# A two-layer diffusion backbone on one core: the opening's modulation rows turned on chip, wider weight runs, and small transfers moved later

## The reference, cut to what matters

```python
def layer(x, xc, c_act, cc_act, lp, cos, sin, with_ctx):
    mod = (c_act @ lp['w_mod'] + lp['b_mod']).reshape(c_act.shape[0], 1, 9, D_MODEL)
    modc = (cc_act @ lp['w_mod'] + lp['b_mod']).reshape(9, D_MODEL)
    m = lambda i: mod[:, :, i]
    mc = lambda i: modc[i]
    ada = lambda t, g, shift, scale: rms_norm(t, g) * (1 + scale) + shift
    x = x + 0.5 * m(2) * ffn(ada(x, lp['norm_ffn1'], m(0), m(1)), 'ffn1')
    xc = xc + 0.5 * mc(2) * ffn(ada(xc, lp['norm_ffn1'], mc(0), mc(1)), 'ffn1')
...
```

## Time and profile before

| | before |
|---|---|
| median of 3 executions | 2305.62 us |
| the profiled execution, its own time | 2308.61 us |
| its span in the profile | 2306.9 us |
| PE busy | 2197.4 us (95%) |
| DVE, ACT, POOL busy | 1472.5, 1006.0, 566.4 us |
| mean DMA rate over the span | 147 GB/s |

### The profile page before, as it was taken

One profiled execution on the slowest core, in us unless ns is written; L12 is line 12 of the kernel. 1 busy time (PEld: TensorE's weight loads), 2 busy tenths in 40 slices (PEclk: granted clock), 3 DMA queues, 4 the chain that ended last, 5 costly groups with the idle time before them and its releaser, 6 DMA issues. The chain is left out here.

```text
span 2306.9 us, 32947 instructions
## 1 busy us (share of the span) xinstructions
PE 2197.4 (95%) x12449; PEld 1851.6 (80%) x12449; DVE 1472.5 (64%) x2102; ACT 1006.0 (44%) x1575; POOL 566.4 (25%) x575
## 2 busy tenths in 40 slices
PE   4999999999999989999999999999999999988998
PEld 3788888977766767888888898888888778788997
DVE  1887786685577546776666675445459658675554
ACT  3544444543455532554334453222245456644443
POOL 2356555340000011243344420000015001110000
PEclk8899999999999999999999999999999999999999
DMA  9566566443333335555555465445545445565663
GB/s 282 155 176 181 159 188 182 140 119 89 101 101 92 99 95 161 149 174 155 146 145 174 126 176 146 142 143 146 154 121 135 119 113 149 147 188 146 181 178 117
DMA packets 501153, 339.76 MB, mean 147 GB/s; under 512 B 13434, under 2 KB 476774, under 8 KB 500870
## 3 DMA queue, kind: packets, MB, share of 16 engines
q1 hardware_dynamic: 470528, 238.06, 36.6%
q0 software_dynamic: 29024, 95.43, 14.6%
q10 hardware_dynamic: 1446, 4.18, 0.6%
HBM read 325.98 MB, written 12.42 MB: 147 GB/s over the span
## 5 line engine op out<-in xcount | busy, mean ns | idle before, releaser
L666 DVE TENSOR_TENSOR w_lo<-raw,w_hi 128x1024 fp32r<-128x1024 f32 (+1 forms) x444 | 582.2, 1312 | 557.1 <-PE bank L706 362.9
L656 ACT ACTIVATE w_hi<-raw 128x1024 fp32r<-128x1024 f32 (+1 forms) x444 | 462.0, 1041 | 707.2 <-PE bank L701 367.3
L700 PE MATMUL bank<-h_hi,w_hi 128*128 128x512 f32 (+1 forms) x1856 | 646.9, 361 | 10.8 <-DVE h_lo L1540 10.8
L701 PE MATMUL bank<-h_lo,w_hi 128*128 128x512 f32 (+1 forms) x1856 | 638.8, 356 | 0.0
L700 PEld LDWEIGHTS bank<-h_hi,w_hi 128*128 128x128 f32 x1856 | 353.2, 190 | 63.1 <-issue 12.7
L706 PE MATMUL bank<-h_hi,w_lo 128*128 128x512 f32 (+1 forms) x1856 | 394.3, 355 | 5.1 <-DVE w_lo L666 5.1
L701 PEld LDWEIGHTS bank<-h_lo,w_hi 128*128 128x128 f32 x1856 | 353.7, 191 | 48.5 <-issue 0.5
L706 PEld LDWEIGHTS bank<-h_hi,w_lo 128*128 128x128 f32 x1856 | 313.1, 189 | 54.5 <-DVE w_lo L666 5.9
L700 PE MATMUL bank<-inner_hi,w_hi 128*128 128x256 f32 (+1 forms) x896 | 272.8, 328 | 11.9 <-DVE inner_lo L1603 11.5
L701 PE MATMUL bank<-inner_lo,w_hi 128*128 128x256 f32 (+1 forms) x896 | 269.4, 324 | 0.0
L700 PEld LDWEIGHTS bank<-inner_hi,w_hi 128*128 128x128 f32 x896 | 170.1, 190 | 31.3 <-DVE inner_lo L1603 15.7
(11 more groups left out here) (243 smaller groups left out, 2934.2 us busy)
## 6 DMA issues: line engine op xcount, KB each, us to landing
wm<-in_w_mod_dram POOLq DMA_DIRECT2D x128, 512.0 KB, 4.3
raw<-in_w_in_dram SPq DMA_DIRECT2D x108, 512.0 KB, 4.0
raw<-in_ffn_w_gate_dram SPq DMA_DIRECT2D x88, 512.0 KB, 4.3
raw<-in_ffn_w_up_dram SPq DMA_DIRECT2D x88, 512.0 KB, 4.0
raw<-in_ffn_w_down_dram SPq DMA_DIRECT2D x88, 512.0 KB, 3.8
raw<-in_ffn_w_down_dram SPq DMA_DIRECT2D x32, 384.0 KB, 3.5
raw<-in_w_out_dram SPq DMA_DIRECT2D x24, 512.0 KB, 3.9
raw<-in_w_mod_dram SPq DMA_DIRECT2D x16, 512.0 KB, 6.5
```

The source lines that it names most:

```text
L656: act.activation(w_hi[n % 2][:, 0:unit.rows, :], raw[unit.slot][:, 0:unit.rows, :], ACT.Copy).then_inc(hi_made, 1)
L666: dve.tensor_tensor(w_lo[n % 2][:, 0:unit.rows, :], raw[unit.slot][:, 0:unit.rows, :], w_hi[n % 2][:, 0:unit.rows, :].bitcast(F32), ALU.su ...
L700: pe.matmul(psum, w_hi[s][:, row0 + k, :], hi, start=(k == 0), stop=False)
L701: mm = pe.matmul(psum, w_hi[s][:, row0 + k, :], lo, start=False, stop=False)
```

## The change

1. The 16 modulation units are cut the other way: a unit is 256 rows of `w_mod` by 512 columns, in runs of 2 KB. `modulation` makes two f32 matmuls of 512 columns from it instead of eight of 128. Group `i` now writes PSUM bank 4 or 5 in turn.
2. `copy_modulation` copies a group to one half of `scores`. `turn_modulation(i)` turns and sums that group with four matmuls, whose right-hand side is a new constant `pick2` of two columns, straight into bank 7. The stores to DRAM and the load back are gone. Groups 0 to 2 are turned behind the second unit of the next group, group 3 at the end. In bank 7 the two streams of a chunk now lie side by side.
3. The token chunks come as 2, 3, 3 and 0 per group instead of 2, 2, 2, 2. The sums of squares, the roots and both reciprocals are placed ahead of the last modulation values.
4. DVE's second weight split is placed inside the first normalisation.
5. The load of the large constants is issued after the first `up` part of the first feed-forward block. The eight bias-row transfers are issued one at a time among the `wm` loads, after pieces 19, 23, ... 47.
6. POOL begins its `wm` loads when the last group is turned. The first block of constants grows by ten columns (`pick2`, `pick8`).

```diff
+for _name, _w in (("ident", 128), ("ones", 128), ("pick2", 2), ("pick8", 8), ("blockones", 128), ...
-FIRST_CONSTS = CONST_COLS["ones"][1]
+FIRST_CONSTS = CONST_COLS["pick8"][1]
+    put("pick2", (p % 32 == np.arange(2)[None, :]).astype(np.float32))
...
-            return range(2 * i, 2 * i + 2)
+            return (range(0, 2), range(2, 5), range(5, 8), ())[i]
...
+        def row_bank(i):
+            return bank[4 + i % 2]
+        def mod_col(chunk, st):
+            return 2 * chunk + st
... SP
-                    stage(first["mod"], MOD_FIRST, lambda j: [((0, DC), columns(w_mod, 0, j * P))])
+                    for j in range(MOD_FIRST):
+                        unit = units[first["mod"] + j]
+                        if j >= SLOTS:
+                            sp.wait_ge(unit_done, j - SLOTS + 1)
+                        sp.dma_start(raw[unit.slot][:, :, :].rearrange("p r c -> p (r c)").rearrange("p (k n) -> p k n", k=2),
+                                     w_mod[0].rearrange("(k p) n -> p k n", p=P)[:, 2 * (j % 4):2 * (j % 4) + 2, j // 4 * 4 * P:(j // 4 + 1) * 4 * P]
+                                     ).then_inc(loaded[unit.slot], 16)
... PE
-                for k in range(DC):
+                for k in (2 * j, 2 * j + 1):
                     rows = slice(32 * (k % 4), 32 * (k % 4) + 32)
-                    mm = pe.matmul(bank[7][rows, j * P:(j + 1) * P], cact[:, k, :], raw[unit.slot][:, k, :],
-                                   start=(k < 4), stop=(k >= 4))
+                    mm = pe.matmul(row_bank(i)[rows, :], cact[:, k, :], two[:, k % 2, :], start=(k < 4), stop=(k >= 4))
...
+            def turn_modulation(i):
+                pe.wait_ge(mod_copied, i + 1)
+                for q in range(GROUP):
+                    c = mod_col(4 * i + q, 0)
+                    mm = pe.matmul(bank[7][:, c:c + 2], scores[:, i % 2, q * P:(q + 1) * P], const("pick2"), start=True, stop=True)
+                mm.then_inc(mod_turned, 1)
...
                         for j in range(4):
-                            modulation(*at(first["mod"], j, i), j, i or None)
+                            modulation(i, j)
+                            if j == 1 and i > 0:
+                                turn_modulation(i - 1)
+                            if j == 1 and i == MOD_FIRST // 4 - 1:
+                                for st in range(2):
+                                    sum_squares((0, 1), st)
...
-                    for st in range(2):
-                        sum_squares((0, 1), st)
-                    turn_modulation(0, "in")
+                    turn_modulation(MOD_FIRST // 4 - 1)
... ACT
-                act.activation(mod_row[:, :], bank[7][:, :], ACT.Copy).then_inc(mod_copied, 1)
+                act.activation(scores[:, i % 2, :], row_bank(i)[:, :], ACT.Copy).then_inc(mod_copied, 1)
...
+                        if i == MOD_FIRST // 4 - 1:
+                            for st in range(2):
+                                norm_root((0, 1), st)
...
-                    const_loads.done(act.dma_start(cst[:, FIRST_CONSTS:CONSTS], consts[:, FIRST_CONSTS:CONSTS]), "all")
...
                 for part in range(len(PARTS)):
                     up(l, 1, part, TOK)
+                    if l == 0 and part == 0:
+                        const_loads.done(act.dma_start(cst[:, FIRST_CONSTS:CONSTS], consts[:, FIRST_CONSTS:CONSTS]), "all")
... DVE
-                    for s in range(2):
-                        split_lo(dve, s)
+                    for st in range(2):
+                        norm_invert((0, 1), st)
+                    split_lo(dve, 0)
                     modulation_vectors(0, "in")
-                norm_block((l, 1), range(2) if l == 0 else range(1, 2))
+                    for st in range(2):
+                        for k in range(DC + 1):
...
+                            if (st, k) == (0, 1):
+                                split_lo(dve, 1)
... POOL
-            with pool.Fori(0, MOD_FIRST // 4) as i:
-                store_modulation(0, i * 4, i)
-            load_modulation()
-            for l in range(LAYERS):
-                for h in range(4):
...
+                if groups[0] == 0:
+                    pool.wait_ge(mod_turned, MOD_FIRST // 4)
...
+                    if (l, ffn) == (0, 1) and i % 4 == 3 and 16 <= i < 48:
+                        write_bias_row(i // 4 - 4)
```

79 lines of the change are left out of this document (36 added, 43 removed).

## The result

The changed kernel took 2292.2 us (median of 4 runs, 2289.2 to 2293.9) against 2305.5 us for the kernel before in the same series (4 runs, 2305.2 to 2307.4). The ratio is 0.9935, with a 95% interval of 0.9923 to 0.9947. The kernel is faster by 13.3 us in the medians; the ratio alone gives 15.0 us, its interval 12.2 to 17.8 us. The forecast was 2287.0 us, a gain of 18.7, with a range of 2280 to 2297. Sign and range hold; the medians gained 5.4 us less than forecast.

A forecast was written before the change was run, and what follows sets the result against it. PE, busy 95% of the span, was taken as the bound, so only its waiting before the first product could be saved: 14.7 + 0.5 + 3.5 = 18.7 us, from 2305.6 to 2287 us, range 2280 to 2297.

The forecast's parts named there:

- The trip and the tail: Last modulation matmul to first product: without the DRAM trip it shrinks from T + 20.5 to T + 5.8, gaining 14.7 us.
- T: End of the opening's last modulation matmul, 42.96 us before; forecast between 37.3 and 40.1, taken as 39.5, 3.5 us earlier.
- a denser PE should see more of 2.4: Opening, 14 to 42 us: PE runs more at 2.4 GHz; at half and half, overlapped, its work takes 23.6 us.
- The way to T: Modulation loads from the first unit at 13.94 us: fifteen shorter gaps save 5.7 us, with up to 2.8 given back.
- The doubled cost of a unit on PE: A modulation unit becomes two 512-column matmuls side by side: 1.71 us at 1.2 GHz, 0.86 at 2.4; before 1.08 and 0.65.
- The first pair: First pair of products, paced by DVE: the second reciprocal leaves (1.74 us), the second split enters (1.18), gaining 0.5 us.
- The moved transfers: Constants and bias rows moved beside later products: put at no cost, bounded at -1 to +4 us.
- no overlap of neighbours: Rival: neighbouring modulation units don't overlap on PE at 1.2 GHz; T 59.1, 2306.6 us, no difference; chance 0.04.
- Wider runs bring nothing: Rival: 2-KB runs load no faster; T stays at 43.0 plus 0.6, gain 14.6, 2291 us; chance 0.13.
- PE bounds the opening, at 1.2 GHz: Rival: PE's work, units overlapping, sets T at 45.4, 2.5 us later; gain 12.7, 2293 us; chance 0.13.
- No `wm` piece was late: Rival: in the first feed-forward block bias transfers starve `wm` loads (pieces 20 to 50); 2310 us or more; chance 0.03.
- Later stretches as long as before: Sign to look for: stretches after the opening keep their length, so the opening's saving reaches the end unshortened.

The follow-up runs named there:

- third profile: The changed kernel run and profiled once more, unaltered, beside both kernels' repeats: median 2291.1 us, ratio 0.9926 to the kernel before.
- seven profiles: Kernels alike up to T: changed kernel three times, moved transfers put back, DVE's vectors before its first weight split, two added-reciprocal delays; T 38.42 to 44.13 us.
- four groups: Changed kernel with each unit's two 512-column matmuls cut into four of 256 columns over four column groups: 2292.1 us, ratio 0.9932.
- the second of before: The kernel before, unaltered, run and profiled again: median 2306.9 us, own time of the profiled execution 2307.15 us.
- nine variants: The nine altered versions of the changed kernel (work order, run length, column groups, transfers or DRAM trip put back, added delays): 2291.4 to 2300.6 us.
- trip back: Changed kernel with the modulation rows again stored to DRAM and loaded back, one turn following: 2300.6 us, ratio 0.9969 to the kernel before.
- the large delay: Changed kernel with four further reciprocals on DVE between first weight split and modulation vectors, 7.0 us planned: 2299.8 us, ratio 0.9967 to before.

## Why the prediction was right, and where it was off

- **The trip and the tail** (14.7 us of the 18.7): right. The tail was forecast at T + 5.8 and measured at T + 5.91, 5.92 and 5.70 in the three profiles. Inside it one sentence was wrong: "The root (with its table load) and the sums go ahead of T and cost the tail nothing." The sums stand so close to T that the reciprocals ended 2.2 us behind it, and the vectors began at T + 3.40 instead of T + 2.9. The last turn was done at T + 1.79, at the higher clock, where T + 2.55 was put. The way from vectors to first product took 2.51 us where 2.9 was put, so the sum came out, in part by luck.
- **T** (3.5 us): the forecast of 39.5 is one of the values that occur (39.52 in the third profile), but not the whole of it. In the first profile T was 42.78 and the step gave 0.2 us; over seven profiles it gave 43.40 - 40.46 = 2.9 us (their median T is 39.75). The step that failed in the first profile is "a denser PE should see more of 2.4". PE fell to the lower level in two of seven, just when it freed no buffers.
- **The way to T** was off, and that the sum of it came near is luck. The forecast left the first unit at 13.94 us and took 5.7 us out of the fifteen gaps, with up to 2.8 given back. Measured, the first unit came at 11.69 us in the mean of the seven, 2.35 earlier than the 14.04 of before (13.94 and 14.14), which no term of the sum held; from there to T it took 28.77 us for 29.36, so the pace gave 0.6. I took 355 GB/s for 2-KB runs; the rows show 325 and 237 in the first profile and 296 in the third from 24 us on, at a DMA share of 0.90 or less. The queue could do more, 357 GB/s with four groups. In the changed kernel PE was busy 7.41 us of 8 from 12 us on; that it then holds back the loads is argued from these rows. The doubled cost of a unit on PE was 1.05 us at 2.4 GHz for 0.86 forecast. Its worth in T is some 1.3 us as far as seen (37.92 in the one profile of four groups, against 39.27 in the five at the full clock, which themselves spread over 1.7 us).
- **The first pair** (0.5 us): right in its own rows, and gone behind them. From the first product to the end of the pair's last `h_lo` it was 79.96 - 63.45 = 16.51 us before and 64.36 - 48.69 = 15.67 us after, 0.8 less. But from the first product to the first root mark it was 354.1 us before and after, so nothing of it was left there.
- **The moved transfers** (0, between -1 and +4): right. Putting them back changed the median by 0.8 us, inside the scatter.
- **The rivals**: "no overlap of neighbours" falls (two units in 1.07 us). "Wider runs bring nothing" falls as a mechanism, though the first profile's T looked like it. "PE bounds the opening, at 1.2 GHz" came nearest in T, 42.8 and 44.1 against its 45.4 in two of seven profiles, but not in its mechanism: the clock stood at the lower level for some 7 us only, and PE still waited for loads. No `wm` piece was late.
- **Later stretches as long as before**: this is the term that was put at nothing and was not, and the second part of the shortfall. They were as long up to the middle mark within the scatter, and not behind it. The changed kernel's first execution led the first of before by 14.71, 16.75 and 14.87 us at the three marks, and the second of before by 15.97, 14.49 and 13.46. From the middle to the last mark before took 946.13 and 946.98 us, the changed kernel 948.01, 948.01 and 949.62, and its nine variants 949.46 to 953.08.

The sum of the opening as measured is 2.9 + 14.9 = 17.8 us (mean tail of before 20.7, of after 5.8), close to 18.7. All 14 runs of the changed kernel have a median of 2291.9 us, and before had medians of 2305.5 to 2307.9, so the gain in time is 13.6 to 16.0 us. What is left, some 2 to 4 us, lies behind the first product. From there to the end the two executions of before took 2245.2 and 2242.4 us, and the three of the changed kernel 2245.3, 2245.4 and 2248.0. The marks say where: between the middle and the last the three took 2.0 us more in the mean than the two of before. PE's waiting there was no longer, some 34 us in each; for its 5822 or 5823 matmul records it was busy 905.88 and 906.64 us before, and 908.65, 908.66 and 910.30 after. Between ACT's last two table loads, about the last 167 us of that way, PE's 1359 records took 162.71 us in the first execution of before and 163.73 in the first of the changed kernel, both at a granted clock of 1.00, so a microsecond of it doesn't show in the granted clock. Its cause stays open. It is not that an earlier start makes the rest longer: nothing is lost up to the first mark, and trip back and the large delay, with first products at 54.58 and 51.21, are as long from the middle to the last mark as the earliest kernels. That before's two profiles were short by chance can't be excluded, but they are the two shortest of fourteen. The nine variants took 2.4 us more again there, in the mean, than the three profiles of the changed kernel; this is part of why the earliest first products (44.33 and 43.08 us) show no gain in time, and it is as unexplained.

## What to carry to other kernels

When load buffers are freed by the engine that also does the side work, read in order of time when each load is asked for: in two of seven executions a block of other work, at the lower clock, emptied the queue (19 and 14 GB/s). But spreading that block filled PE instead and gained nothing on the executions at the full clock, so weigh both limits before moving work. Price a restructured load with what it costs the consumer too, here 1.05 us for 0.64 per unit. When a gain is missing at the end, follow it over marks in the program: here it was whole at 400 us. And before explaining 2 or 3 us in a kernel that keeps PE 95% busy, profile the unaltered kernels a second time: identical code put the same matmul anywhere in a range of 5.7 us.
